# Feed-forward loops of two engines written out, one activation table for Ln and Exp, and work moved into the down product

## Chip, cores and metric

One core of one Trainium2 chip. The metric is the device time of one execution in microseconds (us), median of several. The profile is of one execution.

## What is computed

Two stacks of two layers each on one sequence of 256 tokens, width 1024, all in float32. Each layer is feed-forward, mixer, feed-forward; the mixers are windowed attention beside gated linear attention (stack 0, both layers), a linear recurrence beside causal attention (stack 1, layer 0), and compressed, selected and windowed attention (stack 1, layer 1). The parts of the reference that the change touches, abridged:

```python
def rmsnorm(x, g):                       # 12 norms, 2 final ones, and those inside mixers
    return x * lax.rsqrt(jnp.mean(x * x, axis=-1, keepdims=True) + EPS) * g

# stack 0, feed-forward (inner width 2816)
x = x + 0.5 * (silu(h @ w_gate) * (h @ w_up)) @ w_down      # h = rmsnorm(x, g)

# stack 1
mod = (silu(c) @ mod_w[l] + mod_b[l]).reshape(B, 9, D)
h = modulate(rmsnorm_2(x, norm_g[l, 0]), mod[:, 0], mod[:, 1])
x = x + 0.5 * mod[:, 2][:, None, :] * swiglu_2(h, w1, w2)

# linear recurrence of stack 1, layer 0
log_a = -LRU_C * r * jax.nn.softplus(-lam)
# windowed attention of stack 0: scores + na_bias + mask
```

## The kernel before

x, h and the activations lie transposed in SBUF, features on partitions, tokens along the free axis. Every weight block passes through a ring of two `slot` tiles (128 x 2048 floats): SyncE loads it, ScalarE copies it rounded into `slot_hi` (`split_hi`, L805, two halves), VectorE takes the rest into `slot_lo` (`split_lo`, L1117), and TensorE multiplies three times (`three`, L390 to L392): hi by hi, lo by hi, hi by lo. A load waits on `lo_ready` for the split of the slot two before it.

The order of each engine's work is written out by hand, one block for each engine, held together by counting semaphores. `Seen` keeps the counts; `loop` turns a body into a hardware loop whose counts depend on the turn.

A feed-forward (eight in all, numbered 0 to 7 in the order of the run; two for each layer) has two parts.

- Hidden: 22 slots, 48 matmuls each. ScalarE `gate` takes Silu of the gate half (L849) and splits the slot two ahead; VectorE `hidden` multiplies (L1216), splits and makes `act_hi` and `act_lo`. Both are loops of 10 turns of two slots, and the last two slots are written out, since the slots behind them are half slots of the down product. ScalarE's turn begins with a one-element Silu (L854), so that the table is loaded in every turn. TensorE's loops are not changed.
- Down: 8 output chunks j, two half slots each (11 of the 22 blocks, 33 matmuls). VectorE: `split_both(0)`, `residual(j)` (L1246, x += half of the product), `split_both(1)`, `add_squares` (L1131, the running sum for the next norm). ScalarE splits and squares (L864). Three loop turns of two chunks, the rest written out.

Then `norm_sum` sums over partitions on TensorE (L426, L431), `keep_warm` runs 16 matmuls that nobody reads (L438), and `rstd_of` makes the reciprocal root as exp(-0.5 ln(mean + eps)): Ln at L810, Exp at L811. `norm_table` (L904) runs a one-element Ln ahead of time. VectorE scales x (L1167), ScalarE rounds h (L830, L832), VectorE makes `h_lo` (L1175, L1178) and splits slot 1; TensorE's first product follows h chunk by chunk.

Modulation, the product of `mod_w` with the condition vector, has 144 chunks of 128 x 1024, 24 (a group) in each of feed-forwards 0 to 5. SyncE loads chunk c into one of two `mod_raw` tiles when chunk c - 2 is read (`load_mod`, L294); VectorE multiplies and sums (`mod_chunk`, L1185): 22 of them in the hidden part, the last two behind it, then `mod_group` (L1196 to L1199), all ahead of the first split of the down product. SyncE loads chunks 20 to 25 of the group (the last two belong to the next) between the half slots of j = 0, 1 and 2.

The attention bias of stack 0 (`na_bias`) is loaded in four parts in the down product of feed-forwards 0 and 2, behind j = 1, 3, 5 and 7. POOL waits for all four (one semaphore) and adds the mask in 16 instructions (L372). Softplus for the recurrence, 25 instructions on four columns (`lru_softplus`, from L1351), stands in the mixer of layer 0 between the two halves of the output's norms; the gated linear attention's Ln and Exp are at L1024 and L1028.

## Time and profile before

| | |
|---|---|
| median of 3 runs | 2339.55 us (2336.26 to 2340.13) |
| the profiled execution | 2333.04 us, span 2331.2 us |
| granted TensorE clock, mean | 0.966 |
| busy, share of the span | PE 94%, PEld 89%, DVE 65%, ACT 50%, POOL 2% |
| DMA | 426 MB, 183 GB/s in the mean |

PE is TensorE's matmuls and PEld its weight loads, DVE is VectorE, ACT ScalarE, POOL GpSimd and SP SyncE. A matmul of 128 x 256 counts 0.28 us as busy while the next one begins 0.12 us after it; the busy share is therefore no measure of how near the engine is to its peak, and the places where it is idle, or where its clock is low, are what is to be read.

### The profile page before, as it was taken

Reading aid. Unit: us, or ns where it says so; the run is one execution under the profiler, and the core shown is the slowest. Engines: PE = TensorE matmul, PEld = TensorE weight load, DVE = VectorE, ACT = ScalarE, POOL = GpSimd, SP = SyncE. Lnnn points to the kernel's source line nnn. Section 1 sums busy time; section 2 is a strip of 40 time slices with the busy share of each in tenths; the row PEclk is TensorE's granted clock in tenths of the full one; section 3 lists DMA queues with packets and bytes.
Section 4 is the critical chain, followed back from the end, with each engine's and each line's share of the span. In section 5 each row is a group of like instructions: output and inputs, shape, how many; then the busy total and the mean of one; then the engine's idle time right before and its main releaser. Section 6 shows DMA issues by size and latency. Waiting matters only on the chain.

```text
span 2331.2 us, 43089 instructions
## 1 busy us (share of the span) xinstructions
PE 2188.9 (94%) x16944; PEld 2077.2 (89%) x16944; DVE 1518.2 (65%) x2582; ACT 1154.8 (50%) x1852; POOL 35.9 (2%) x38
## 2 busy tenths in 40 slices
PE   9989978999999997899889999899899999999998
PEld 8989957999999995899879999699899998658998
DVE  7766386775776648677467656677655555785554
ACT  5434565543553456554355445655345444454543
POOL 0002000000000200000000000000000000000000
PEclk9999989999999998999989999899999999699999
DMA  7865412775677541277548654257655454203544
GB/s 274 302 237 186 176 55 85 273 263 190 221 274 237 189 164 51 100 271 261 184 167 275 241 178 149 81 205 271 197 175 183 165 196 146 73 1 119 185 167 142
DMA packets 78053, 426.09 MB, mean 183 GB/s; under 512 B 9696, under 2 KB 10464, under 8 KB 47632
## 3 DMA queue, kind: packets, MB, share of 16 engines
q1 hardware_dynamic: 77968, 424.95, 53.2%
q8 instruction: 54, 0.88, 0.2%
q14 instruction: 31, 0.25, 0.0%
HBM read 423.86 MB, written 1.05 MB: 182 GB/s over the span
## 4 chain that ended last, share of the span: by engine, by line
PE 81%; DVE 11%; ACT 4%; issue 2%; DMA 1%; DVEq 0%; ACTq 0%
PE bank L390 24%; PE bank L391 24%; PE bank L392 24%; DVE slot_lo L1117 3%; DVE h L1167 2%; DMA mod_raw<-in_mod_w_dram 1%; ACT slot_hi L805 1%; ACT L811 1%; PE bank L717 1%; PE bank L418 1%; DVE room L1390 1%; PE bank L420 1%; PE bank L419 1%; PE bank L519 1%; DVE room L1402 1%
## 5 line engine op out<-in xcount | busy, mean ns | idle before, releaser
L390 PE MATMUL bank<-h_hi,slot_hi 128*128 128x256 f32 x3552 | 1015.1, 286 | 30.9 <-DVE slot_lo L1117 11.5
L1117 DVE TENSOR_TENSOR slot_lo<-slot,slot_hi 128x1024 fp32r<-128x1024 f32 (+1 forms) x728 | 791.0, 1108 | 363.1 <-ACT slot_hi L805 359.7
L391 PE MATMUL bank<-h_lo,slot_hi 128*128 128x256 f32 x3552 | 1007.5, 284 | 0.0
L392 PE MATMUL bank<-h_hi,slot_lo 128*128 128x256 f32 x3552 | 1007.2, 284 | 0.0
L805 ACT ACTIVATE slot_hi<-slot 128x1024 fp32r<-128x1024 f32 (+1 forms) x728 | 660.1, 957 | 316.8 <-PE bank L392 303.7
L390 PEld LDWEIGHTS bank<-h_hi,slot_hi 128*128 128x128 f32 x3552 | 684.1, 193 | 42.2 <-issue 29.5
L391 PEld LDWEIGHTS bank<-h_lo,slot_hi 128*128 128x128 f32 x3552 | 684.4, 193 | 1.8 <-issue 1.7
L392 PEld LDWEIGHTS bank<-h_hi,slot_lo 128*128 128x128 f32 x3552 | 684.2, 193 | 0.0
L390 PE MATMUL bank<-act_hi,slot_hi 128*128 128x256 f32 x1408 | 402.8, 286 | 34.0 <-DVE slot_lo L1117 34.0
L391 PE MATMUL bank<-act_lo,slot_hi 128*128 128x256 f32 x1408 | 401.5, 285 | 0.0
L392 PE MATMUL bank<-act_hi,slot_lo 128*128 128x256 f32 x1408 | 401.1, 285 | 0.0
L849 ACT ACTIVATE room<-bank 128x256 f32<-128x256 f32 x176 | 67.8, 385 | 495.4 <-PE bank L392 494.0
L390 PEld LDWEIGHTS bank<-act_hi,slot_hi 128*128 128x128 f32 x1408 | 271.9, 193 | 35.2 <-DVE slot_lo L1117 35.2
L391 PEld LDWEIGHTS bank<-act_lo,slot_hi 128*128 128x128 f32 x1408 | 271.9, 193 | 0.0
L392 PEld LDWEIGHTS bank<-act_hi,slot_lo 128*128 128x128 f32 x1408 | 271.6, 193 | 0.0
L1216 DVE TENSOR_TENSOR room<-room,bank 128x256 f32<-128x256 f32 x176 | 74.2, 422 | 190.9 <-ACT room L849 190.5
L1185 DVE SCALAR_TENSOR_TENSOR mod_raw<-mod_raw,cond 128x1024 f32<-128x1024 f32 x144 | 175.6, 1220 | 22.5 <-DMA mod_raw<-in_mod_w_dram 22.3
L854 ACT ACT_TABLE_LOAD x70 | 89.8, 1283 | 1.3
L898 ACT ACTIVATE room<-bank 128x512 f32<-128x512 f32 x37 | 22.1, 596 | 114.4 <-PE bank L392 85.9
L1225 DVE TENSOR_TENSOR act_lo<-room,act_hi 128x256 f32 (+1 forms) x176 | 73.7, 419 | 0.0
L923 ACT ACTIVATE room<-room,stats 128x15 f32<-128x15 f32 (+1 forms) x144 | 61.2, 430 | 14.0 <-DVE stats L1309 10.9
L418 PE MATMUL bank<-slot_hi,h_hi 128*128 128x256 f32 (+1 forms) x192 | 56.0, 292 | 0.0
(222 smaller groups left out, 1678.5 us busy)
## 6 DMA issues: line engine op xcount, KB each, us to landing
slot<-in_slots_dram SPq DMA_DIRECT2D x236, 1024.0 KB, 5.0
slot<-in_wd_dram SPq DMA_DIRECT2D x128, 704.0 KB, 4.1
mod_raw<-in_mod_w_dram SPq DMA_DIRECT2D x144, 512.0 KB, 5.2
room<-in_na_bias_dram SPq DMA_DIRECT2D x8, 512.0 KB, 5.0
x<-in_x_dram SPq DMA_DIRECT2D x1, 1024.0 KB, 5.1
out_dram<-h SPq DMA_DIRECT2D x4, 256.0 KB, 2.4
cond<-in_cond_dram SPq DMA_DIRECT2D x1, 512.0 KB, 9.4
lru_w<-in_lru_w_dram SPq DMA_DIRECT2D x1, 512.0 KB, 6.1
```

Of the source, the lines that this page charges most:

```text
L390: pe.matmul(o, slot_hi[b][:, w:w + P], x_hi, start=first, stop=False, skip_group_check=skip)
L391: pe.matmul(o, slot_hi[b][:, w:w + P], x_lo, start=False, stop=False, skip_group_check=skip)
L392: return pe.matmul(o, slot_lo[b][:, w:w + P], x_hi, start=False, stop=last, skip_group_check=skip)
L418: pe.matmul(o, t_hi, w_hi, start=(k == 0), stop=False)
L805: act.activation(slot_hi[b][:, c0:c1], slot[b][:, c0:c1], ACT.Copy).then_inc(s["hi_ready"], 1)
L849: act.activation(sil[:, b, :], bank[b][:, 0:S], ACT.Silu).then_inc(s["sil_ready"], 1)
L854: link(act.activation(warm[:, 4:5], ones[:, 0:1], ACT.Silu))
L923: last = act.activation(scores[:, i % 3, c:c + n], scores[:, i % 3, c:c + n], ACT.Exp, bias=stats[:, i % 2, k + j:k + j + 1], accum_out=st ...
L1117: ins = dve.tensor_tensor(slot_lo[b][:, c0:c1], slot[b][:, c0:c1], slot_hi[b][:, c0:c1].bitcast(F32), ALU.subtract)
L1185: dve.scalar_tensor_tensor(out=mod_raw[b][:, :], in0=mod_raw[b][:, :], scalar=1.0, in1=cond[:, :], op0=ALU.mult, op1=ALU.mult, accum_out=m ...
L1216: dve.tensor_tensor(act_f[:, b, :], sil[:, b, :], bank[b][:, S:2 * S], ALU.mult).then_inc(s["dve_step"], 1)
L1225: dve.tensor_tensor(lo, act_f[:, b, :], hi.bitcast(F32), ALU.subtract).then_inc(s["act_ready"], 1)
```

## The change

- SyncE: the four bias parts are loaded behind j = 2, 3, 4, 5, each with a semaphore of its own; the first two chunks of the next group at j = 6 and no longer at j = 2.
- POOL masks each part when its own semaphore comes.
- ScalarE: both feed-forward loops are written out. The Silu table is loaded once for each feed-forward; `norm_table` loads the set that holds both Ln and Exp, and is called once more, in the mixer of stack 0 behind its last Silu.
- VectorE: both loops are written out. The last two modulation chunks stand behind the squares of j = 1 and 2, `mod_group` behind those of j = 3, `lru_softplus` behind those of j = 4 in feed-forward 1.

```diff
@@ sync
-                             ...).then_inc(s["bias_ready"], 16)
+                             ...).then_inc(s[BIAS_READY[part]], 16)
                 for j in range(KC):
                     for half in range(2):
                         load_down_slot((ffn * KC + j) * 2 + half)
-                        if j < 3 and ffn < MOD_GROUPS:
+                        if j < 2 and ffn < MOD_GROUPS:
                             load_mod(ffn * MOD_GROUP + FC - 2 + 2 * j + half)
-                    if bias is not None and j % 2 == 1:
-                        load_bias(bias, j // 2)
+                        elif j == 6 and ffn < MOD_GROUPS:
+                            load_mod((ffn + 1) * MOD_GROUP + half)
+                    if bias is not None and 2 <= j < 6:
+                        load_bias(bias, j - 2)
@@ gpsimd
-                pool.wait_ge(s["bias_ready"], seen("bias_ready", 16 * BIAS_PARTS))
                 for head in range(NA_HEADS):
+                    if head % (NA_HEADS // BIAS_PARTS) == 0:
+                        part = BIAS_READY[head * BIAS_PARTS // NA_HEADS]
+                        pool.wait_ge(s[part], seen(part, 16))
@@ scalar, ffn
-                with loop(act, seen, FC // 2 - 1, slot_done=2, act_ready=2, slot0_ready=16, slot1_ready=16, act_step=1):
-
-                    link(act.activation(warm[:, 4:5], ones[:, 0:1], ACT.Silu))
-                    for b in range(2):
-                        gate(b, SLOT)
-                for b in range(2):
-                    gate(b, HALF_SLOT)
+                act.preload_act_table(ACT.Silu)
+                for c in range(FC):
+                    gate(c % 2, SLOT if c < FC - 2 else HALF_SLOT)
                 norm_table()
...
-                with loop(act, seen, KC // 2 - 1, x_ready=2, sum_step=2, slot_done=4, slot0_ready=32, slot1_ready=32) as t:
...
+                for j in range(KC - 1):
+                    for b in range(RING):
+                        act.wait_ge(s["slot_done"], seen("slot_done"))
+                        split_hi(b, HALF_SLOT)
+                    square(j, j % 2)
@@ scalar
             def norm_table():
 
-                link(act.activation(warm[:, 4:5], ones[:, 0:1], ACT.Ln))
+                act.preload_act_table_set("natural_log_exp_and_others")
@@ scalar, mixer1
                     project(n, {6: "s", 8: "w", 9: "w"}.get(n, ""))
+                    if n == 9:
+                        norm_table()
@@ vector, ffn
-                with loop(dve, seen, FC // 2 - 1, sil_ready=2, dve_step=4, hi_ready=4, **per_mod) as t:
-                    for b in range(2):
-                        hidden(t * 2 + b, b, SLOT)
-                for b in range(2):
-                    hidden(FC - 2 + b, b, HALF_SLOT)
+                for c in range(FC):
+                    hidden(c, c % 2, SLOT if c < FC - 2 else HALF_SLOT)
                 clear_sum()
-                if modulation:
-                    for b in range(2):
-                        mod_chunk(FC + b, b)
-                    mod_group(group)
...
-                with loop(dve, seen, KC // 2 - 1, slot_done=4, sq_ready=2, sum_step=2, hi_ready=8) as t:
...
+                for j in range(KC - 1):
+                    split_both(0, HALF_SLOT)
+                    residual(j, j % 2)
+                    split_both(1, HALF_SLOT)
+                    add_squares(1, j)
+                    if modulation and j in (1, 2):
+                        mod_chunk(FC + j - 1, (j - 1) % 2)
+                    elif modulation and j == 3:
+                        mod_group(group)
+                    elif group == 1 and j == 4:
+                        lru_softplus()
@@ vector, mixer1
                 split_mix(0)
-                if layer == 0:
-                    lru_softplus()
```

## Rows read from the trace of the kernel before

**Rows 1.** The page, chain that ended last: share of the span by engine.

```profile
PE 81%; DVE 11%; ACT 4%; issue 2%; DMA 1%; DVEq 0%; ACTq 0%
```

**Rows 2.** Groups by line: busy us, mean ns of one, idle before and its releasers.

```profile
L390 PE MATMUL bank<-act_hi,slot_hi 128*128 128x256 f32 x1408 | 402.8, 286 | 34.0 <-DVE slot_lo L1117 34.0
...
L811 ACT ACT_TABLE_LOAD x16 | 20.5, 1283 | 0.3
```

**Rows 3.** Instructions in time, SyncE and VectorE, feed-forward 0: start us, us.

```profile
149.46 0.33 SPq L294 DMA_DIRECT2D mod_raw<-in_mod_w_dram  x1
...
154.90 1.23 DVE L1185 SCALAR_TENSOR_TENSOR mod_raw<-mod_raw,cond 128x1024 f32<-128x1024 f32 x1 [3.92 <-DMA mod_raw<-in_mod_w_dram]
```

**Rows 4.** Busy by stretch: PE, PEld, DVE, ACT, POOL, granted clock, DMA, GB/s.

```profile
158.70:165.20 6.50, 6.50 (x35) 6.50 (x36) 2.12 (x4) 0.42 (x1) 0.00 (x0) 0.59 0.83 301
```

**Rows 5.** Instructions in time, ScalarE, down products of feed-forwards 0, 5, 6.

```profile
152.76 1.47 ACT L805 ACTIVATE slot_hi<-slot 128x704 fp32r<-128x704 f32 x2 [2.34 <-PE bank L392]
...
165.32 1.48 ACT L805 ACTIVATE slot_hi<-slot 128x704 fp32r<-128x704 f32 x2 [5.81 <-PE bank L392]
...
1663.36 1.47 ACT L805 ACTIVATE slot_hi<-slot 128x704 fp32r<-128x704 f32 x2 [2.34 <-PE bank L392]
...
1677.04 1.47 ACT L805 ACTIVATE slot_hi<-slot 128x704 fp32r<-128x704 f32 x2 [6.05 <-PE bank L392]
...
1869.96 1.48 ACT L805 ACTIVATE slot_hi<-slot 128x704 fp32r<-128x704 f32 x2 [2.35 <-PE bank L392]
1873.95 1.47 ACT L805 ACTIVATE slot_hi<-slot 128x704 fp32r<-128x704 f32 x2 [2.21 <-PE bank L392]
```

**Rows 6.** Instructions in time, VectorE, down product of feed-forward 6.

```profile
1872.40 0.42 DVE L1131 TENSOR_TENSOR sqsum<-sqsum,sq 128x256 f32<-128x256 f32 x1
1874.77 1.70 DVE L1117 TENSOR_TENSOR slot_lo<-slot,slot_hi 128x704 fp32r<-128x704 f32 x2 [1.95 <-ACT slot_hi L805]
```

**Rows 7.** One line of the kernel, L281, the half slots' loads.

```profile
DMA to landing us min/median/max: 3.7/4.1/6.2
```

**Rows 8.** Instructions in time, ScalarE, norm behind feed-forward 1.

```profile
593.50 0.38 ACT L810 ACTIVATE rstd<-bank 128x256 f32<-128x256 f32 x1 [0.85 <-PE bank L431]
593.90 1.28 ACT L811 ACT_TABLE_LOAD   x1
595.19 0.42 ACT L811 ACTIVATE rstd<-rstd 128x256 f32<-128x256 f32 x1
```

**Rows 9.** Instructions in time, TensorE, the same norm and the product behind it.

```profile
593.05 4.00 PE L438 MATMUL bank<-slot_hi 128*128 128x512 f32 x16
...
604.52 0.36 PE L390 MATMUL bank<-h_hi,slot_hi 128*128 128x256 f32 x1 [1.14 <-DVE slot_lo L1117]
```

**Rows 10.** Instructions in time, ScalarE, mixer of stack 0, layer 0.

```profile
361.09 1.28 ACT L1028 ACT_TABLE_LOAD   x1
```

**Rows 11.** Instructions in time, POOL and VectorE, norms behind feed-forwards 0 and 1.

```profile
208.36 15.41 POOL L372 TENSOR_TENSOR room<-room,na_mask 128x256 f32<-128x256 f32 x16 [207.92 <-DMA room<-in_na_bias_dram]
...
209.02 2.23 DVE L1117 TENSOR_TENSOR slot_lo<-slot,slot_hi 128x704 fp32r<-128x704 f32 x2 [0.40 <-ACT slot_hi L805]
...
220.07 2.24 DVE L1167 SCALAR_TENSOR_TENSOR h<-x,gains,rstd 128x256 f32<-128x256 f32 x3 [3.53 <-ACT rstd L811]
...
226.90 1.08 DVE L1178 TENSOR_TENSOR h_lo<-h,h_hi 128x256 fp32r<-128x256 f32 x3
...
595.64 1.28 DVE L1167 SCALAR_TENSOR_TENSOR h<-x,gains,rstd 128x256 f32<-128x256 f32 x3 [3.45 <-ACT rstd L811]
...
600.49 1.09 DVE L1178 TENSOR_TENSOR h_lo<-h,h_hi 128x256 fp32r<-128x256 f32 x3
```

**Rows 12.** Instructions in time, VectorE, softplus in the mixer of layer 0.

```profile
358.46 0.16 DVE L1351 TENSOR_SCALAR lru_c<-lru_c 128x4 f32<-128x4 f32 x1
...
363.21 0.74 DVE L1453 SCALAR_TENSOR_TENSOR h<-bank,gla_gain,room 128x512 f32<-128x512 f32 x1
```

**Rows 13.** The chain that ended last in order of time, its first piece.

```profile
1.46 5.09 issue
```

More of the change, by code:

```diff
@@ L303, in load_bias @@
                 sp.dma_start(na_bias[:, part * heads:part * heads + heads, :],
-                             a["na_bias"][layer, :, part * heads:part * heads + heads, :]).then_inc(s["bias_ready"], 16)
+                             a["na_bias"][layer, :, part * heads:part * heads + heads, :]).then_inc(s[BIAS_READY[part]], 16)
             sp.dma_start(x[:, :, :], a["x"]).then_inc(s["x_loaded"], 16)
@@ L863, in square @@
                     act.wait_ge(s["sum_step"], seen("sum_step"))
[L864 to L876 removed]
+                    act.activation(sq[:, b, 0:S], x[:, j, :], ACT.Square).then_inc(s["sq_ready"], 1)
+                for j in range(KC - 1):
[3 more added lines that the diff above has]
+                    square(j, j % 2)
                 act.wait_ge(s["slot_done"], seen("slot_done"))
@@ L1219, in hidden @@
                     dve.wait_ge(s["dve_step"], value)
-                    hi, lo = (v[:, bass.ds(c, 1), :].rearrange("p a b -> p (a b)") for v in (act_hi, act_lo))
+                    hi, lo = act_hi[:, c, :], act_lo[:, c, :]
                     dve.tensor_copy(hi, act_f[:, b, :]).then_inc(s["dve_step"], 1)
@@ L1235, in ffn @@
                 clear_sum()
-                if modulation:
-                    for b in range(2):
-                        mod_chunk(FC + b, b)
-                    mod_group(group)
                 def residual(j, bk):
                     dve.wait_ge(s["slot_done"], seen("slot_done", 2))
-                    xj = x[:, bass.ds(j, 1), :].rearrange("p a b -> p (a b)")
-                    half = 0.5 if stack == 0 else mod_gate[:, layer, i, bass.ds(j, 1)]
-                    dve.scalar_tensor_tensor(out=xj, in0=bank[2 + bk][:, 0:S], scalar=half, in1=xj,
+                    half = 0.5 if stack == 0 else mod_gate[:, layer, i, j:j + 1]
@@ L1247, in residual @@
+                    dve.scalar_tensor_tensor(out=x[:, j, :], in0=bank[2 + bk][:, 0:S], scalar=half, in1=x[:, j, :],
                                              op0=ALU.mult, op1=ALU.add).then_inc(s["x_ready"], 1)
-                with loop(dve, seen, KC // 2 - 1, slot_done=4, sq_ready=2, sum_step=2, hi_ready=8) as t:
-                    for j in range(2):
-                        split_both(0, HALF_SLOT)
-                        residual(t * 2 + j, j)
-                        split_both(1, HALF_SLOT)
-                        add_squares(1, j)
```

21 lines of the change are left out of this document (3 added, 18 removed).

## The prediction

> **What bounds the kernel now.** I read the page's chain first. The chain that ended last is 81% TensorE and 11% VectorE [rows 1], so the product stream sets the time and only what stops it is worth anything. Next, the groups by line: in the down product TensorE stood idle for 34.0 us, all of it behind a split on VectorE, L1117 [rows 2]. The same view has 16 table loads at L811, one ahead of each Exp of `rstd_of` [rows 2]. Which of these lie on the path is seen in the instructions in order of time, one feed-forward at a time.
>
> I call the half slots of the down product D0, D1, ... (two for each output chunk j). D0 and D1 are split during the last two turns of the hidden loop. D2 can be split only when D0 is used up, so from there on TensorE has one product, 3.8 to 4.0 us, of cover.
>
> In feed-forward 0 SP issues the load of the last modulation chunk at 149.46. VectorE has to read this chunk before it may split D2, and gets it at 154.90 after 3.92 us of idle time for that DMA [rows 3]. There are six such places, so each holds 34.0 / 6 = 5.7 us of idle time in the mean. When TensorE has D2 at last, from 158.7 to 165.2, its mean granted clock is 0.59 [rows 4]: mostly the 1.2 GHz level, behind a stop of nearly 6 us, against 2.4 GHz before.
>
> ScalarE's splits of the half slots show when each product ends, as each waits for the one before. D1 ends by 152.76 and D2 by 165.32, 12.56 us apart; in feed-forward 5 it is 13.68 us (1663.36 to 1677.04) [rows 5]. The four between them have 11.43, 11.85, 12.49 and 10.62 us. Feed-forward 6 has no modulation and is a control made by the kernel itself: 1869.96 to 1873.95, 3.99 us [rows 5].
>
> **The change part by part.**
>
> *The last two modulation chunks.* They are read behind the squares of j = 1 and j = 2, and the group is finished behind j = 3. Both loads are issued as before, by the end of the last hidden turn, and the first read comes two output chunks later, some 14 us; SP, whose next group's loads now stand at j = 6, waits for no read there. So D2 follows D1 as in feed-forward 6. The six intervals sum to 72.63 us; six times 3.99 us is 23.94. Gain 48.7 us, the slow clock behind each stall included.
> What is late next? In feed-forward 6 the squares end at 1872.82, the next split begins at 1874.77 and ends at 1876.47 [rows 6], and TensorE would want it at 1877.77: the products of a pair take 3.99 and 3.82 us, and the second began at 1873.95 [rows 5]. That is 1.95 us of idle time and 1.30 us of slack. A chunk takes 1.23 us [rows 3] and 0.08 us for the accumulator: it fits in the idle time. The group's three small instructions take about 0.7 us and fit too. I cost both at nothing. If the idle time were not there, the slack of 1.30 us would still take the chunk's 1.31, so the upper bound is 0 too.
>
> *The queue on SP.* Each half slot's load is issued when the split two before it ends, and is wanted when that slot's product is over: for D6 in feed-forward 6 issue at 1876.47 [rows 6] and need at 1877.77 + 3.99 = 1881.76, 5.29 us. It lands in 3.7 to 6.2 us, median 4.1 [rows 7]. D4 now follows the last chunk's load more closely, and the bias parts follow D5, D7, D9, D11. Bound: 0 to 0.9 us once in each of six, 0 to 5.5 us. I take 0, since the median has 1.2 us to spare.
>
> *One table for Ln and Exp.* The 16 loads of L811 go, one in each norm; each takes 1.28 us. In feed-forward 1's end the Ln starts at 593.50, the load at 593.90, the Exp at 595.19 [rows 8]: nothing covers it. After it VectorE scales, splits h, then splits slot 1, and TensorE waits for that. What is late next is the warm-up: 16 matmuls from 593.05 for 4.00 us, to 597.05 [rows 9]. The first product takes 5.7 us more, to about 602.8, while the split of slot 1, for which the second product starts at 604.52 after 1.14 us of waiting [rows 9], comes 1.28 us earlier, at about 603.1. So the split is still last and the whole 1.28 us comes back. The load ahead of the Exp at L1028 goes too (361.09, 1.28 us) [rows 10], with the out projection's k = 4 waiting for what follows; there are 2. The load at L1024 is covered by a TensorE sum, and I count it at nothing; at most it is 2 x 1.28 = 2.6 us. The loads inside the hidden loop are covered by ScalarE's waits for products. Sum: 18 x 1.28 = 23.1 us.
> Here a page speaks: by the Trainium skill (ScalarE: Activation LUTs, section What ACT_TABLE_LOAD costs) a switch of sets costs the 1283 ns load and about 1380 ns of drain, 2.66 us. By it the 18 would bring 47.9 us. The row bears out the load alone: between the Ln's 0.38 us and the Exp only 0.03 us are left beside the load [rows 8].
>
> *The bias.* Its parts come after j = 2 to 5 and not 1, 3, 5, 7, and POOL starts on each at its landing. Now POOL's 16 additions run from 208.36 for 15.41 us [rows 11], over the end of feed-forward 0 and its norm. From the first scaling to the last h_lo this norm takes 220.07 to 227.98, 7.91 us; without POOL, in feed-forward 1, 595.64 to 601.58, 5.94 us [rows 11]. Difference 1.97 us, with 0.1 us for the split before it 2.1 us, in two feed-forwards: gain 4.2 us. The additions go to the middle of the down product, where a pair of half-slot splits beside POOL takes 2.23 us against 1.70 [rows 6, 11]. In one output chunk POOL's four additions, 3.9 us, meet about four VectorE instructions of this kind; 0.53 us for the split pair, as much for the squares, some 0.6 for the chunk: 1.7 us against 0.64 left idle and 1.30 of slack. I take 0.5 us for each of the two feed-forwards, 1.0; bounds 0 and 15 (the rival below). Net 3.2 us.
>
> *Softplus.* It runs from 358.46 to 363.21, 4.75 us [rows 12], and only the last 0.2 us lie on the path, as the load at L1028 ends at 362.37 [rows 10] and the Exp of a first half takes some 0.6 more. It goes behind the squares of j = 4 in feed-forward 1: 4.75 and 0.08 us against 1.95 + 1.30 leaves 1.6 us that TensorE waits. Behind the wait of 1.14 us [rows 9] matmuls still began 0.12 us apart, so I add no slow clock. Net cost 1.4 us; bounds -0.2 (it hides in full) and 4.
>
> *Loops written out.* ScalarE and VectorE have slack in each turn, so the branches, the warm-up activations and their loads cover nothing and give nothing. What the longer program costs in fetching instructions the trace doesn't show in steady state: 0 to the rival below. I take 0, as the mixers, written out already, show VectorE no such wait.
>
> Sum: 48.7 + 23.1 + 3.2 - 1.4 = 73.6 us. The profiled execution took 2333.04 us for a span of 2331.2; it would take 2259.4. It is 6.5 us under the median of the three timed runs, 2339.55, so that the median becomes 2265.9.
>
> **The rivals.**
>
> *A. The set doesn't stay.* If the Exp gets its own load again, or another wait on ScalarE takes the place of the load, 23.1 us don't come: 2339.55 - 50.5 = 2289.0. For it: placing loads is not the kernel's work alone. Against it: the kernel's Ln, run ahead today, already saves the Ln a load in the norms (none stands ahead of 593.50). 0.07.
>
> *B. POOL shuts VectorE out.* If a VectorE instruction waits for a whole addition, four of them in an output chunk cost 4 x 0.96 = 3.85 us against 0.64 + 1.30, 1.9 us for each of 8 parts, 15.3 us instead of 1.0: 2280. Against it: the pair of splits lost 0.53 us, not 1.9 [rows 6, 11]. The Trainium skill (SBUF - State Buffer, on the shared port pair) calls it an exclusive lock for which the loser fully blocks; by it B would be likelier than the row makes it. 0.08.
>
> *C. Slower: fetching.* The one long wait at the start of a program that the chain puts down to issue is 5.09 us [rows 13]. Were each of the 32 written-out loops (two in each of eight feed-forwards on two engines) to meet one of 5.1 us, 1.30 us of it taken by slack, 3.8 us each would be 122 us: 2339.55 - 73.6 + 122 = 2388. It decides from 20 such waits on. Against it: VectorE shows no such wait in the mixers. 0.03.
>
> *D. A drain goes with each load.* 2.66 us for each of 18, 24.8 us more: 2241. The 0.03 us of the row speaks against it [rows 8]. 0.03.
>
> **How the numbers follow.** Forecast 0.79: 2265.9, its own range 2254 to 2277 (downwards 2.6 us at L1024, 1.6 of softplus, 1.0 of POOL, 4 for the spread of the runs, 3 for gaps at the loops' branches that no row shows; upwards 5.5 of landing, 2.6 of softplus, 3 of spread). To leave out no more than 2 in 10 the range reaches to B: 2254 to 2283. Faster by over 0.2%, about what a measurement of this kernel can tell from none: all but C, 0.96; within it 0.01, between A and C; slower 0.03.
>
> **What would show it.** In the down product the idle time of TensorE behind L1117 falls from 34.0 us to under 4, and ScalarE's splits after D1 come 3.9 to 4.0 us apart in all eight; no table load stands between Ln and Exp; POOL's additions lie in the down product in four groups; one wait of 1 to 2 us in feed-forward 1 behind softplus. The forecast is wrong if the chunk's read at j = 1 or 2 waits for a DMA, if ScalarE waits for a half slot's landing, or if VectorE's hidden turns grow.

## The result, and the profile after

The changed kernel takes 2266.28 us (median of four, 2261.82 to 2282.78) against 2338.48 us for the kernel before on the same occasion: ratio 0.9707, 95% interval 0.9681 to 0.9733, or 72.2 us less. The forecast was 2265.9 in a range of 2254 to 2283. The profiled execution took 2266.51 us for a span of 2264.5 us, 66.7 us less than the span before.

The page of the changed kernel first: the chain by engine, then groups of instructions (busy time and mean ns of one, then the idle time of the engine before them and what ended it), then the issues of DMAs with the median time to landing.

```profile
PE 83%; DVE 11%; ACT 4%; issue 1%; DMA 1%; DVEq 0%; ACTq 0%
...
L395 PE MATMUL bank<-act_hi,slot_hi 128*128 128x256 f32 x1408 | 396.1, 281 | 2.1 <-DVE slot_lo L1114 1.9
...
L1182 DVE SCALAR_TENSOR_TENSOR mod_raw<-mod_raw,cond 128x1024 f32<-128x1024 f32 x144 | 177.4, 1232 | 0.0
...
slot<-in_wd_dram SPq DMA_DIRECT2D x128, 704.0 KB, 4.1
mod_raw<-in_mod_w_dram SPq DMA_DIRECT2D x144, 512.0 KB, 5.2
```

TensorE's first product of a half slot (L390 before, L395 now) was idle for 34.0 us [rows 2] and is now idle for 2.1. VectorE no longer waits for a modulation chunk at all (L1182, 0.0). The median landing of a half slot is what it was.

The end of feed-forward 1 on ScalarE, in order of time (start, duration; in brackets the idle time before, and what ended it):

```profile
551.59 1.47 ACT L810 ACTIVATE slot_hi<-slot 128x704 fp32r<-128x704 f32 x2 [2.13 <-PE bank L397]
555.49 1.47 ACT L810 ACTIVATE slot_hi<-slot 128x704 fp32r<-128x704 f32 x2 [2.43 <-PE bank L397]
557.27 0.42 ACT L865 ACTIVATE sq<-x 128x256 f32<-128x256 f32 x1 [0.31 <-DVE x L1234]
561.16 1.48 ACT L810 ACTIVATE slot_hi<-slot 128x704 fp32r<-128x704 f32 x2 [3.48 <-PE bank L397]
565.06 1.47 ACT L810 ACTIVATE slot_hi<-slot 128x704 fp32r<-128x704 f32 x2 [2.43 <-PE bank L397]
...
574.59 0.38 ACT L815 ACTIVATE rstd<-bank 128x256 f32<-128x256 f32 x1 [0.85 <-PE bank L436]
575.01 0.42 ACT L816 ACTIVATE rstd<-rstd 128x256 f32<-128x256 f32 x1
```

The splits of half slots lie 3.9 us apart but for one interval of 5.67 us (555.49 to 561.16): the stop behind softplus, 1.77 us. The Exp follows the Ln in 0.42 us, from start to start, where it was 1.69 with the load between them [rows 8].

One measure is used throughout below: the time from one Ln of `rstd_of` to the next on ScalarE, which cuts the program into 15 stages. Grouped and summed (us; "again" is a later traced execution of the changed kernel, that of experiment 10 below; "forecast" are the terms of the sum put where they were expected):

| stages | before | forecast of difference | changed | difference | changed, again | difference |
|---|---|---|---|---|---|---|
| feed-forwards 0 to 5 | 1229.3 | -53.8 | 1176.5 | -52.8 | 1176.0 | -53.3 |
| mixers of stack 0, both parts | 343.2 | -12.1 | 334.3 | -8.9 | 330.9 | -12.3 |
| mixer of stack 1, layer 0 | 133.1 | -1.3 | 134.6 | +1.5 | 131.9 | -1.2 |
| norm between the stacks | 11.5 | -1.3 | 10.1 | -1.3 | 10.1 | -1.3 |
| feed-forwards 6 and 7, last mixer | 593.5 | -3.8 | 589.6 | -4.0 | 589.7 | -3.8 |
| ahead of the first Ln and behind the last (span less the rest) | | -1.3 | | -1.4 | | -1.5 |
| span | 2331.2 | -73.6 | 2264.5 | -66.7 | 2257.8 | -73.4 |

The execution called "again" meets the forecast of the span (2331.2 - 73.6 = 2257.6) within 0.2 us, and each group within 0.5. It is the fastest of all 14 executions of the changed kernel, and the profiled execution of the kernel before (2333.04 us) is faster than every timed one of that kernel, so this compares a fast execution with a fast one. A third trace of the changed kernel (experiment 1) has a span of 2263.5 us, 67.7 us less than before. The first misses the forecast by 6.9 us, 3.2 in the mixers of stack 0, 2.8 in the mixer of stack 1 and 1.0 in the feed-forwards. The two larger ones can be seen in windows (busy time of PE, PEld, DVE, ACT and POOL, then the mean granted clock, the share of the DMA engines and GB/s). Changed kernel, the attention of stack 0, layer 0, and the mixer of stack 1, layer 0:

```profile
328.70:343.00 14.30, 10.34 (x57) 7.11 (x56) 6.29 (x10) 6.29 (x14) 0.00 (x0) 0.76 0.01 2
...
1422.60:1435.20 12.60, 12.60 (x40) 6.80 (x38) 5.79 (x13) 8.18 (x26) 0.00 (x0) 0.67 0.01 1
```

The same work in the kernel before:

```profile
340.00:352.00 12.00, 8.04 (x60) 5.60 (x59) 6.30 (x10) 7.58 (x15) 0.00 (x0) 1.00 0.00 1
...
1476.00:1486.00 10.00, 10.00 (x42) 5.59 (x41) 5.66 (x13) 8.27 (x26) 0.00 (x0) 0.89 0.01 2
```

The same number of matmuls, within three, took 2.3 and 2.6 us longer at a clock of 0.76 and 0.67 against 1.00 and 0.89. This is no work that the change touches. The stage of the first window takes 133.92 us in this trace, 131.00 in that of experiment 1, 132.55 in "again" and 130.4 in the shortest of all. The stage of the second window takes 134.6 us here, 134.3 in experiment 1 and 131.9 in "again". So the first stretch changes from one execution to the next; the second came back once and was gone once. Over all runs below it is in four of the ten traces with the new table and in none of the three with the old one, too few to show whether the change makes it likelier. How large such stretches get is told further down.

### The profile page after: what moved, and what is told of

Same layout as the page of the kernel before. It is cut to its first block, busy times and chain, and to the rows that moved or that the text cites. A ratio compares the mean times of both kernels' runs of the same rounds, so it can differ in the third digit from the quotient of the medians.

```text
span 2264.5 us, 40255 instructions
## 1 busy us (share of the span) xinstructions
PE 2171.2 (96%) x16944; PEld 2062.6 (91%) x16944; DVE 1524.5 (67%) x2582; ACT 1025.2 (45%) x1672; POOL 41.0 (2%) x38
## 4 chain that ended last, share of the span: by engine, by line
PE 83%; DVE 11%; ACT 4%; issue 1%; DMA 1%; DVEq 0%; ACTq 0%
PE bank L395 24%; PE bank L397 24%; PE bank L396 24%; DVE slot_lo L1114 3%; DVE h L1164 2%; ACT slot_hi L810 1%; PE bank L722 1%; PE bank L524 1%; PE bank L423 1%; DVE room L1379 1%; PE bank L425 1%; PE bank L424 1%; DVE room L1391 1%; DMA slot<-in_wd_dram 1%; PE bank L436 1%
## 5 line engine op out<-in xcount | busy, mean ns | idle before, releaser
L395 PE MATMUL bank<-h_hi,slot_hi 128*128 128x256 f32 x3552 | 1010.5, 284 | 15.5 <-DVE slot_lo L1114 6.9
L395 PEld LDWEIGHTS bank<-h_hi,slot_hi 128*128 128x128 f32 x3552 | 683.1, 192 | 22.2 <-issue 13.8
L395 PE MATMUL bank<-act_hi,slot_hi 128*128 128x256 f32 x1408 | 396.1, 281 | 2.1 <-DVE slot_lo L1114 1.9
L396 PE MATMUL bank<-act_lo,slot_hi 128*128 128x256 f32 x1408 | 395.6, 281 | 0.0
L397 PE MATMUL bank<-act_hi,slot_lo 128*128 128x256 f32 x1408 | 395.5, 281 | 0.0
L395 PEld LDWEIGHTS bank<-act_hi,slot_hi 128*128 128x128 f32 x1408 | 265.3, 188 | 3.0 <-DVE slot_lo L1114 2.9
L397 PEld LDWEIGHTS bank<-act_hi,slot_lo 128*128 128x128 f32 x1408 | 265.3, 188 | 0.0
L396 PEld LDWEIGHTS bank<-act_lo,slot_hi 128*128 128x128 f32 x1408 | 265.3, 188 | 0.0
L1182 DVE SCALAR_TENSOR_TENSOR mod_raw<-mod_raw,cond 128x1024 f32<-128x1024 f32 x144 | 177.4, 1232 | 0.0
L1222 DVE TENSOR_TENSOR act_lo<-room,act_hi 128x256 fp32r<-128x256 f32 x176 | 73.5, 418 | 0.0
L424 PE MATMUL bank<-slot_lo,h_hi 128*128 128x256 f32 (+1 forms) x192 | 54.6, 284 | 0.0
```

The costliest lines, as they stand in the source:

```text
L395: pe.matmul(o, slot_hi[b][:, w:w + P], x_hi, start=first, stop=False, skip_group_check=skip)
L396: pe.matmul(o, slot_hi[b][:, w:w + P], x_lo, start=False, stop=False, skip_group_check=skip)
L397: return pe.matmul(o, slot_lo[b][:, w:w + P], x_hi, start=False, stop=last, skip_group_check=skip)
L424: pe.matmul(o, t_hi, w_lo, start=False, stop=False)
L1182: dve.scalar_tensor_tensor(out=mod_raw[b][:, :], in0=mod_raw[b][:, :], scalar=1.0, in1=cond[:, :], op0=ALU.mult, op1=ALU.mult, accum_out=m ...
L1222: dve.tensor_tensor(lo, act_f[:, b, :], hi.bitcast(F32), ALU.subtract).then_inc(s["act_ready"], 1)
```

## Experiments

The theory: stalls on VectorE and table loads on the path are what the change takes away, each independently, and loops and POOL matter little. Rivals: the loops written out, rather than the chunks, shorten the down product; POOL holds VectorE up; the granted clock, not the stall, is what comes back.

**1. The changed kernel once more**, the comparison for the three that follow. No edit.

> The changed kernel once more, for how much its own time and trace vary. In the first trace 2.9 us in the attention of stack 0, layer 0, and 2.8 us in that of stack 1, layer 0, were lost at a lower granted clock, with the same work. If this depends on where in the chip's own rhythm the work falls, the new trace has such stretches at other places or none, and the time is 2260 to 2283 us with the clock lower where the time is longer. If the change itself causes them, they are at the same two places again.

2268.1 us, ratio 0.9695 (0.9668 to 0.9722), span 2263.5. The first result repeats. Of the two places in question, the attention of stack 0, layer 0, got its 2.9 us back, and the mixer of stack 1, layer 0, did not (134.27 us): the expectation had no case for one of each, and this trace decides neither way. It also has something that the first does not, a stop of TensorE in feed-forward 4, which is told under the queue on SP.

**2. The order of the modulation chunks put back.**

```diff
                 clear_sum()
+                if modulation:
+                    for b in range(2):
+                        mod_chunk(FC + b, b)
+                    mod_group(group)
...
                     add_squares(1, j)
-                    if modulation and j in (1, 2):
-                        mod_chunk(FC + j - 1, (j - 1) % 2)
-                    elif modulation and j == 3:
-                        mod_group(group)
-                    elif group == 1 and j == 4:
+                    if group == 1 and j == 4:
                         lru_softplus()
```

> The changed kernel with one part undone: the last two modulation chunks and their group are read ahead of the down product again; all else as changed. My account of the time: the six stops of the down product come back whole, with their slow clock, 48.7 us as summed from the trace of the kernel before, so about 2315 us, and TensorE idle by about 34 us behind VectorE's splits in the down product. Rival, that writing the loops out or the other moves carried part of that gain: clearly less than 40 us comes back.

2314.34 us, ratio 0.9874 (0.9845 to 0.9903): 46.2 us above experiment 1. The groups of this run have the stall back, with a DMA ahead of it:

```profile
L395 PE MATMUL bank<-act_hi,slot_hi 128*128 128x256 f32 x1408 | 402.4, 286 | 31.6 <-DVE slot_lo L1114 31.6
...
L1182 DVE SCALAR_TENSOR_TENSOR mod_raw<-mod_raw,cond 128x1024 f32<-128x1024 f32 x144 | 175.7, 1220 | 19.7 <-DMA mod_raw<-in_mod_w_dram 19.5
```

The six stages are 1218.6 us long, 42.1 more than in the first trace of the changed kernel and 40.9 more than in that of experiment 1. Of the other stages the last mixer is 12.8 us longer than in experiment 1, at a lower granted clock, so 46.2 us by the medians is not the price of the chunks alone. Well over 40 us of the stages is theirs: the chunks carry the gain. Of the 31.6 us of idle time 1.5 are the stop behind softplus in feed-forward 1, and 30.1 the six stops of the chunks.

**3. The loops alone.** The kernel before with ScalarE's and VectorE's feed-forward loops written out and the Silu table loaded once for each; tables of the norms, chunks, bias and softplus as before.

```diff
-                with loop(act, seen, FC // 2 - 1, slot_done=2, act_ready=2, slot0_ready=16, slot1_ready=16, act_step=1):
-                    link(act.activation(warm[:, 4:5], ones[:, 0:1], ACT.Silu))
-                    for b in range(2):
-                        gate(b, SLOT)
-                for b in range(2):
-                    gate(b, HALF_SLOT)
+                act.preload_act_table(ACT.Silu)
+                for c in range(FC):
+                    gate(c % 2, SLOT if c < FC - 2 else HALF_SLOT)
```

> The kernel before with nothing but the feed-forward loops of ScalarE and VectorE written out (one Silu table load for a feed-forward): chunks, bias, softplus and the Ln activation as before. My account: both engines have slack in every turn, so within 3 us of the kernel before, about 2338. Rival, the branches and warm-up activations were on the path: 10 us or more faster. Rival, the longer program costs fetches: slower.

2336.07 us, ratio 0.9979 (0.9968 to 0.9990). Not nothing: 3.4 us by the medians, 2 to 7 by the interval. The groups by line say where:

```profile
L390 PE MATMUL bank<-act_hi,slot_hi 128*128 128x256 f32 x1408 | 402.2, 286 | 31.4 <-DVE slot_lo L1107 31.4
```

The idle time falls from 34.0 us to 31.4. By ScalarE's splits the six intervals from the end of D1 to that of D2 sum to 68.1 us and not 72.6 [rows 5], and in experiment 2, which has the loops written out too, to 67.0. So the loops seem to have lengthened the very stall that the chunks made. This is likely rather than shown: of the six intervals four are shorter (by 2.4, 1.5, 0.7 and 0.4 us), one is the same and one 0.3 longer, and the six stages as a whole are only 2.7 us shorter than before (1226.6 us). Of the 48.7 us forecast for the chunks some 3 to 5 belong to the loops, when they are written out first. The profiled execution (2340.69 us) is nevertheless longer than that of before, by stretches of low clock in the mixers.

**4. The old tables.** The changed kernel with the one-element Ln in `norm_table` and without its new call in the mixer.

```diff
-                act.preload_act_table_set("natural_log_exp_and_others")
+                link(act.activation(warm[:, 4:5], ones[:, 0:1], ACT.Ln))
...
-                    if n == 9:
-                        norm_table()
```

> The changed kernel with the table change undone: a one-element Ln ahead of each norm as before, and no call behind the last Silu of the mixer. My account: 16 loads between Ln and Exp and 2 in the gated linear attention come back at 1.28 us each, 23.1 us, less 1.1 us in the first norm, where the trace of the changed kernel shows that the condition's Silu hid the gain: about 22 us slower than the changed kernel, 2288. Rival, a drain goes with each load: about 46 us slower. Rival, the warm-up matmuls were the next bound: clearly less than 15 us.

2290.67 us, ratio 0.9784 (0.9758 to 0.9811), 22.6 us above experiment 1. ScalarE at the end of feed-forward 1 in this run:

```profile
580.86 0.39 ACT L815 ACTIVATE rstd<-bank 128x256 f32<-128x256 f32 x1 [0.85 <-PE bank L436]
581.26 1.28 ACT L816 ACT_TABLE_LOAD   x1
582.56 0.42 ACT L816 ACTIVATE rstd<-rstd 128x256 f32<-128x256 f32 x1
```

The stage of feed-forward 1 is 198.22 us with the old tables and 196.92 without, feed-forwards 6 and 7 are 196.92 and 196.95 against 195.63 and 195.68: 1.27 to 1.30 us each, the load and no more. A drain beside each load, 2.66 us for both as in rival D, is not there.

**5. The bias put back** behind j = 1, 3, 5, 7, with one semaphore for all parts.

```diff
-                    if bias is not None and 2 <= j < 6:
-                        load_bias(bias, j - 2)
+                    if bias is not None and j % 2 == 1:
+                        load_bias(bias, j // 2)
...
+                pool.wait_ge(s["bias_ready"], seen("bias_ready", 16 * BIAS_PARTS))
                 for head in range(NA_HEADS):
-                    if head % (NA_HEADS // BIAS_PARTS) == 0:
-                        part = BIAS_READY[head * BIAS_PARTS // NA_HEADS]
-                        pool.wait_ge(s[part], seen(part, 16))
```

> The changed kernel with the bias undone: four loads behind j = 1, 3, 5, 7, one semaphore, POOL's 16 additions at the end of the down product. My account: the norm behind feed-forwards 0 and 2 is longer by 1.97 us each, and the down products of both lose their small stops beside POOL (0.7 and 0.35 us in the first trace): about 3.1 us slower than the changed kernel, 2270. The spread between runs is as large, so the stage from the norm's Ln to the attention's, 130.5 us where no slow clock falls into it, decides: 132.4 in both. Rival, POOL's additions block VectorE in the down product as long as they run: the down products become faster than the norm becomes slower, and this kernel is faster.

2283.36 us, ratio 0.9747 (0.9717 to 0.9776): far more than expected by the time, and the two stages in question take 136.9 and 137.0 us, not 132.4. The trace divides it. The norm ahead of the first mixer, ScalarE's Ln and its first two copies out of the product (changed kernel, then this run):

```profile
209.80 0.38 ACT L815 ACTIVATE rstd<-bank 128x256 f32<-128x256 f32 x1 [0.85 <-PE bank L436]
...
219.17 0.60 ACT L893 ACTIVATE room<-bank 128x512 f32<-128x512 f32 x1 [1.13 <-PE bank L397]
...
225.65 0.60 ACT L893 ACTIVATE room<-bank 128x512 f32<-128x512 f32 x1 [3.99 <-PE bank L397]
```

```profile
209.39 0.39 ACT L812 ACTIVATE rstd<-bank 128x256 f32<-128x256 f32 x1 [0.85 <-PE bank L433]
...
221.14 0.60 ACT L890 ACTIVATE room<-bank 128x512 f32<-128x512 f32 x1 [0.49 <-PE bank L394]
...
228.26 0.60 ACT L890 ACTIVATE room<-bank 128x512 f32<-128x512 f32 x1 [4.63 <-PE bank L394]
```

From the Ln to the first copy 11.75 us against 9.37, to the second 18.87 against 15.85: POOL over the norm costs 3.0 us here, where the forecast had 2.1. The forecast was read with the old table, and there it holds: the second copy comes 19.10 us behind the Ln in the kernel before and 17.13 with the old tables and the early bias (experiment 4), 1.97 us apart. The two changes lean on each other. Together they bring 19.10 - 15.85 = 3.25 us for each of these norms, where 2.1 and 1.28 were forecast.

The mixer's first part is 136.9 us, another 3.5 us more, and 17 us of it ran at a granted clock of 0.80; the changed kernel's first trace, with 133.92 us and 3.5 above the shortest, has a like stretch at the same place. The last mixer is 13 us longer. In the down product the late bias saves little: feed-forward 2 takes 195.29 us against 195.50. So POOL's additions beside the splits cost about 0.2 us, not 0.5, and the price of rival B (15 us) is false. The median of the times says nothing more about the bias, as the clock's share in it is the larger one.

**6. Softplus put back** into the mixer.

```diff
-                    elif group == 1 and j == 4:
-                        lru_softplus()
...
                 split_mix(0)
+                if layer == 0:
+                    lru_softplus()
```

> The changed kernel with softplus back in the mixer. My account: feed-forward 1 loses its stop of 1.77 us, and the norms of the mixer's output become 0.2 us longer: 1.5 us faster than the changed kernel, 2266 or so; in the trace feed-forward 1 takes 195.2 us from Ln to Ln, not 196.9, and the second half of the mixer 34.2 where no slow clock falls into it. Rival, softplus would now stand on the mixer's path with its whole length, since the table loads beside it are gone: 38.7.

2274.36 us, ratio 0.9716 (0.9692 to 0.9740), of which 13 us are again the last mixer's clock. The stages that the edit touches: feed-forward 1 takes 195.17 us against 196.92, the stop of 1.75 us gone; the mixer's second part takes 38.33 against 33.95. VectorE and ScalarE in that part of this run:

```profile
350.32 0.16 DVE L1351 TENSOR_SCALAR lru_c<-lru_c 128x4 f32<-128x4 f32 x1
350.39 0.74 DVE L1440 SCALAR_TENSOR_TENSOR h<-bank,gla_gain,room 128x512 f32<-128x512 f32 x1
```

```profile
347.44 1.15 ACT L1025 ACTIVATE room<-room 128x512 f32<-128x512 f32 x2
```

The pair of Exp began at 347.44, the first of them was over at about 348.0 (half of 1.15), and VectorE was not free for it until 350.39: softplus holds the path up for 2.35 us. With the old tables it didn't, since the load at L1028 kept the Exp back about as long [rows 10, 12]. The other 2 us of the 38.33 are slow clock. It begins while TensorE has nothing to do for want of this h:

```profile
350.00:352.00 2.00, 0.00 (x0) 0.00 (x0) 1.90 (x7) 0.10 (x1) 0.00 (x0) 0.90 0.00 0
352.00:358.00 6.00, 4.36 (x20) 4.36 (x21) 2.92 (x7) 2.44 (x3) 0.00 (x0) 0.50 0.00 0
```

A shorter such stretch stands at this place in three traces without softplus there, and costs 1.5 us (35.45 against 33.95), so one trace doesn't show whose the 2 us are. With them the rival of the expectation (38.7) was nearly met. My step "only the last 0.2 us on the path" held for the kernel before and not for the changed one.

**7. Softplus in thirds** behind j = 4, 5 and 6, and no second Silu load in the first feed-forward.

```diff
-                    elif group == 1 and j == 4:
-                        lru_softplus()
+                    elif group == 1 and j in (4, 5, 6):
+                        lru_softplus(j - 4)
...
-                act.preload_act_table(ACT.Silu)
+                if not stack == layer == i == 0:
+                    act.preload_act_table(ACT.Silu)
```

> The changed kernel with softplus cut in three, behind the squares of j = 4, 5, 6 (9, 8 and 8 instructions of 0.2 us, each within 1.95 us of idle time), and without the second load of the Silu table in feed-forward 0, behind the condition's Silu. My account: 1.77 us in feed-forward 1 (195.2 us from Ln to Ln) and about 1.1 us in feed-forward 0, 2.9 us faster than the changed kernel, 2265. Rival for the second: the first products of feed-forward 0 wait for h and not for the gate, and it brings nothing.

2261.0 us (five, 2256.62 to 2265.96), ratio 0.9679 (0.9662 to 0.9696). ScalarE's splits in the same place:

```profile
551.01 1.48 ACT L810 ACTIVATE slot_hi<-slot 128x704 fp32r<-128x704 f32 x2 [2.43 <-PE bank L397]
552.40 0.40 ACT L866 ACTIVATE sq<-x 128x256 f32<-128x256 f32 x1
554.92 1.47 ACT L810 ACTIVATE slot_hi<-slot 128x704 fp32r<-128x704 f32 x2 [2.13 <-PE bank L397]
```

3.91 us between splits: the stop is gone, and feed-forward 1 takes 195.17 us, 1.75 less. Feed-forward 0 takes 196.44 against 196.8 to 197.3.

**8. Filler on VectorE**, to measure the slack that hides the moved chunks: two more products of 128 x 1024 behind the squares of j = 1 to 5 in feed-forward 6, three in feed-forward 7. They are extra work whose output nobody reads.

```diff
+                    if group >= MOD_GROUPS and 1 <= j < 6:
+                        for f in range(2 if group == 6 else 3):
+                            link(dve.scalar_tensor_tensor(out=mod_raw[0][:, :], in0=cond[:, :], scalar=1.0, in1=cond[:, :],
+                                                          op0=ALU.mult, op1=ALU.mult))
```

> The changed kernel with idle work for VectorE behind the squares of j = 1 to 5 in the last two feed-forwards, which have no modulation: 2 multiplications of 128 x 1024 each time in feed-forward 6, 3 in feed-forward 7, 1.3 us for one. My account: VectorE has 1.95 us of idle time and 1.30 us of slack there. 2.6 us fit and feed-forward 6 stays at 195.6 us from Ln to Ln; 3.9 us are 0.65 too many, five times, so feed-forward 7 takes about 3.3 us more, 199. Rival, no slack beyond the idle time: 3.3 us more in feed-forward 6 and 9.8 in 7.

2266.96 us (two executions), ratio 0.9698. Feed-forward 6, with 2.5 us of filler in each of five chunks, takes 195.63 us, as without. Feed-forward 7 takes 198.03, 2.35 more; three were not hidden. So between 2.5 and 3.7 us of VectorE time lie free in each output chunk, and a modulation chunk of 1.3 us is well inside. The size for three was expected a little too high (3.3): the splits show a delay of 0.78 us three times, not 0.65 five times, as what is late in one chunk is made up in part in the next.

**9. The stop kept warm.** Experiment 2, with products of ones on TensorE in the stop behind D1, in feed-forwards 0 to 5. TensorE's first two output chunks are written out for it in all eight; feed-forwards 6 and 7 keep their 195.63 and 195.68 us, so this alone changes nothing.

```diff
+                        if first and j == 1 and b == 0:
+                            for _ in range(WARM_STOP):            # 11
+                                pe.matmul(bank[5][:, 0:S], ones[:, 0:P], ones[:, :], start=True, stop=True)
                         pe.wait_ge(s["lo_ready"], seen("lo_ready"))
```

> The kernel with only the order of the last two modulation chunks taken back (2314.3 us when measured, 46 to 48 above the changed kernel), and with eleven products of ones (128x256) put on TensorE in the stop between the first and the second half of the down product of ffns 0 to 5; they compute nothing that is used. In the kernel before, the stop itself idled 34.0 us in those stages and the whole loss was forecast at 48.7; the difference of 14.6 us, some 2.4 us a stage, was put to the lower granted clock behind the stop. If the slow clock follows from the idle stop, the products keep the clock and each of the six stages is about 2.4 us shorter: about 2300 us, and TensorE's second turn no longer takes 6.5 us but 3.9. If the clock is lower for another reason (the activity before the stop, the whole chip), the time stays at 2314 within 3 us. If the products last longer than the stop they add their excess, at most 1 us a stage.

2302.86 us, ratio 0.9840 (0.9808 to 0.9872), 11.5 us less than experiment 2. The windows of feed-forward 0 around the stop, experiment 2 and then this one:

```profile
157.00:164.00 7.00, 6.74 (x38) 6.74 (x39) 2.48 (x5) 0.76 (x2) 0.00 (x0) 0.63 0.71 254
```

```profile
157.00:164.00 7.00, 6.54 (x56) 6.53 (x56) 3.18 (x6) 1.74 (x3) 0.00 (x0) 1.00 0.75 248
```

38 matmuls at 0.63 against 56 (few of them the warm ones) at 1.00, in the same 7 us. The six stages sum to 1208.3 us against 1218.6: 10.3 us come back. So the cost of the six stops is 30.1 us of idle time and some 10 to 12 us behind them, of which at least 10.3 are low clock, and the low clock follows from the idleness. The 14 us that I had put to the clock was too much; in feed-forwards 1, 2 and 3 it is 0.9 to 1.2 us each, in 0, 4 and 5 1.8 to 3.0.

The Trainium skill (TensorE: Matmul & The Clock Gate, Part 1) says the same of the mechanism, that an idle TensorE falls to half its clock and must be busy for a while to get it back.

**10 and 11. The changed kernel and the version of experiment 7, side by side**, on one chip.

> The changed kernel once more, on the same chip as the next run and as its comparison: 2266 to 2268 us, with 33.95 to 34 us in the second part of the mixer wherever the clock stays up, and single attention stages 1.5 to 3.5 us above their shortest, not in the same places as before.

> The version with the softplus of ffn 1 spread in thirds over the down product, once more on the same chip as the changed kernel. If the stop of TensorE in ffn 1 (1.77 us) and the like stop in ffn 0 are what the move costs, this version is 2 to 3 us faster than the changed kernel beside it (2263 to 2265 against 2266 to 2268). If its 2261.0 us of the first time came from luck with the clock, the two are the same within 1 us.

2263.41 us (2259.81 to 2283.0) and 2263.21 (2256.28 to 2278.16), six executions of each. By the medians nothing tells them apart, so this expectation was missed. In the traces feed-forward 1 takes 196.94 and 195.16 us, feed-forward 0 takes 196.93 and 196.68: 2.0 us saved, and the attention of stack 0, layer 1, loses 3.5 us again (130.42 against 133.89). The lowest of 14 executions of the changed kernel over all occasions is 2259.81 us, that of 11 of the version in thirds 2256.28. I hold it to be some 2 us faster by its stages; a median of six can't show it.

## Why the prediction was right, point by point

**The modulation chunks, 48.7 us: right in the sum**, as that of two causes that I had taken for one. Experiment 2 gives 42.1 us by stages and 46.2 by medians, and experiment 3 gives 2.7 us by stages and 3.4 by medians to the loops. The control, feed-forward 6, was the right one: D2 behind D1 takes 3.91 us there. In the modulated feed-forwards it takes 4.0 to 5.3 us, and the next product is shorter by nearly as much: ScalarE waits for a landing, and the slack takes it.

**The idle time and the slack on VectorE, 1.95 and 1.30 us: right.** Experiment 8 puts the free time in each chunk between 2.5 and 3.7 us; I had 3.25.

**The queue on SP, taken at 0: right in the first trace, wrong in how near it is, and 1.8 us in another.** The prediction named "if ScalarE waits for a half slot's landing" as a sign of being wrong, and splits 3.9 to 4.0 us apart as one of being right. The first came and the second did not. The waits on ScalarE in the changed kernel (sum, times, longest):

```profile
ACT slot_hi L810 <- DMA slot<-in_wd_dram: 34.7, 14, 3.5
```

In 14 places a half slot lands after TensorE has freed its buffer. In feed-forward 4 the split stands 1.4 us late:

```profile
1282.34 0.41 ACT L865 ACTIVATE sq<-x 128x256 f32<-128x256 f32 x1
1286.29 1.48 ACT L810 ACTIVATE slot_hi<-slot 128x704 fp32r<-128x704 f32 x2 [3.54 <-DMA slot<-in_wd_dram]
```

TensorE has a whole product of cover at that point and does not stop (of its 2.1 us of idle time 1.5 lie behind softplus and 0.4 in feed-forward 0). In the trace of experiment 1 the same split is later:

```profile
1285.78 1.47 ACT L810 ACTIVATE slot_hi<-slot 128x704 fp32r<-128x704 f32 x2 [4.92 <-DMA slot<-in_wd_dram]
```

Its half slot landed after 7.9 us, where the slowest in the kernel before took 6.2. TensorE then stopped for 1.5 us, and feed-forward 4 took 197.47 us against 195.63 in "again". The forecast's bound for one feed-forward was 0.9. The median of the landings was no measure of this; the slowest ones were late, and only the cover made the term 0 where it was 0.

**One table, 23.1 us: right**, 22.6 by the medians of experiment 4 against 1. What I had "counted at nothing, at most 2.6", the load at L1024, is worth 0.2 us each: the mixer's second part takes 36.74 us with the old tables (experiment 4, layer 1) and 33.96 with the new ones, both at full clock throughout, 2.78 us where 2.56 was forecast. From the kernel before it fell by 3.6 and 3.2 us, but there 3.4 us of each ran at the lower clock. In the first feed-forward the load brought back 0.7 to 1.2 us (198.02 us in experiment 4 against 197.32 and 196.83) and not 1.28. Another load also came in there. ScalarE in the changed kernel:

```profile
21.24 1.28 ACT L848 ACT_TABLE_LOAD   x1
22.53 1.06 ACT L848 ACTIVATE cond<-cond 128x1024 f32<-128x1024 f32 x1
23.61 1.28 ACT L857 ACT_TABLE_LOAD   x1
24.90 0.38 ACT L854 ACTIVATE room<-bank 128x256 f32<-128x256 f32 x1
```

The Silu table is loaded twice, behind each other: the explicit load is issued although the table is in place. Before, the one-element Silu stood there and needed none. The version of experiment 7 leaves it out in this place, and feed-forward 0 is 0.4 to 0.9 us shorter there, 0.3 in experiment 11 beside 10. The Trainium skill (ScalarE: Activation LUTs, section What ACT_TABLE_LOAD costs) has 1.28 us for the load, which all traces show, and a drain of about 1.38 us beside it, which none does: 0.01 and 0.02 us are left between Ln, load and Exp in experiment 4.

**The bias, net 3.2 us: right within 1, counted beside the old table.** POOL now works in the down product. POOL's four additions and VectorE in feed-forward 0 of the changed kernel, each instruction by itself:

```profile
162.13 0.99 POOL L377 TENSOR_TENSOR room<-room,na_mask 128x256 f32<-128x256 f32 x1 [161.69 <-DMA room<-in_na_bias_dram]
163.08 1.38 POOL L377 TENSOR_TENSOR room<-room,na_mask 128x256 f32<-128x256 f32 x1
164.42 0.92 POOL L377 TENSOR_TENSOR room<-room,na_mask 128x256 f32<-128x256 f32 x1
165.31 1.71 POOL L377 TENSOR_TENSOR room<-room,na_mask 128x256 f32<-128x256 f32 x1
```

```profile
162.44 1.43 DVE L1114 TENSOR_TENSOR slot_lo<-slot,slot_hi 128x704 fp32r<-128x704 f32 x1
163.79 0.96 DVE L1128 TENSOR_TENSOR sqsum<-sqsum,sq 128x256 f32<-128x256 f32 x1
164.67 1.75 DVE L1182 SCALAR_TENSOR_TENSOR mod_raw<-mod_raw,cond 128x1024 f32<-128x1024 f32 x1
```

Each VectorE instruction beside POOL loses 0.5 us (1.43 against 0.89, 0.96 against 0.42, 1.75 against 1.23), as forecast, and the free time in each output chunk takes nearly all of it. The gain at the norm was 1.97 us beside the old table and 3.0 beside the new one, against 2.1; the cost in the down product 0.2 against 0.5.

The rows also show how the time is lost. The two engines end in turn: POOL at 163.12, VectorE at 163.87, POOL at 164.46, VectorE at 164.75, POOL at 165.34, VectorE at 166.43, POOL at 167.02. Behind each end of VectorE's, POOL needs 0.6 us more, nearly the 0.73 that a whole addition takes alone (in the kernel before, with VectorE idle):

```profile
217.44 0.73 POOL L372 TENSOR_TENSOR room<-room,na_mask 128x256 f32<-128x256 f32 x1
```

VectorE's modulation chunk ends 1.08 us behind POOL's addition, where it takes 1.23 alone. So each waits for the other's whole instruction, and the exclusive lock of the Trainium skill (SBUF — State Buffer, "Who interferes with whom") agrees with these rows. Rival B had the mechanism right and the price wrong: a VectorE instruction waits for one addition, part of which had run already, 0.5 us and not 0.96, so that four cost about 2.1 us against 1.94 us of free time.

**Softplus, a cost of 1.4 us: half wrong.** The stop is 1.77 us (forecast 1.6). But what the move gives back in the mixer is 2.35 us and not 0.2, so the move gains about 0.6 us, and up to 2.6 if the low clock behind it is its own. The step that failed is "the last 0.2 us lie on the path, as the load at L1028 ends at 362.37": I costed this edit against the kernel before, although another edit of the same change takes that load away. Terms that lean on each other must be costed in the kernel that holds both.

**The loops, nothing: wrong by 3.4 us alone, right in the sum**, if, as it seems, the gain lies in the stall that goes anyhow. I had listed 3 us for gaps at the branches in the lower end of the range.

**The rivals.** A is false (no load between Ln and Exp), B is false in its price (experiment 5) and not in its mechanism, C is false (no wait for fetching appears; feed-forwards 6 and 7 are 1.28 us shorter and nothing else), D is false (experiment 4).

**From the span to the median.** I added the 6.5 us by which the profiled execution of before was under its median. The changed kernel's profiled execution is at its median, and 6.9 us of the forecast gain are missing from its trace, by stretches of low clock. So these two cancelled by luck: the sum of the parts is 73.4 us in the fastest execution, 66.7 and 67.7 in the two other traces, and 72.2 between the medians. That the median came within 0.4 us of the forecast is in part luck of this kind.

## What to carry to other kernels

Look for a twin of the stage without the suspected work: feed-forward 6, with no modulation, gave the price of the stall, the clock included, better than any sum of instructions. An item that is read from DMA on an engine with a hand-written order belongs where a whole product is left as cover, in pieces smaller than the idle time of that place (1.3 us hides, 4.8 us stops TensorE for 1.8, thirds of it hide again). And where a change has several parts, cost each in the kernel that has the others: one part took away the load that had hidden another, and made the start of the norm meet more of POOL's additions.

## What the runs showed of the chip that I had not expected

How long the granted clock stays low differs between executions of one program, on stages that are the same code. The last mixer takes 198 to 200 us in eight of thirteen traces, 204 in one, and 211 in four. In all thirteen a stretch at the lower level begins 75 to 78 us into that stage, so the place is the same; it lasts 24 us in the eight, 34 in the one, and 44 or 51 in the four; in one of the latter, experiment 5, two whole windows of 25 us lie at the lower level:

```profile
1950.00:1975.00 25.00, 23.48 (x65) 14.54 (x65) 18.88 (x57) 13.90 (x54) 0.00 (x0) 0.50 0.19 70
1975.00:2000.00 25.00, 25.00 (x73) 14.38 (x72) 11.70 (x39) 6.11 (x27) 0.00 (x0) 0.50 0.00 1
```

The same 13 us may stand between the two clusters of times of the changed kernel (2260 to 2270 us and 2275 to 2283 us; those at the ends had mean granted clocks of 0.979 and 0.968); the trace of none of the long ones was taken, so that this is inferred. What sets the length of such a stretch stays open; the long ones fall in the mixers, while feed-forwards 6 and 7 were 195.6 and 195.7 us long in every trace with the new tables and no filler. A stop of 4.7 to 6.7 us in a dense stream is another matter: in all six places of the kernel before and of experiments 2 and 3, the product behind it was late by more than the idle time. One of 1.77 us left it: behind it the products came 3.90 us apart, as before.
